# Forty instead of thirty-two tokens by gathered rows in the expert layer of a fused two-block kernel

## The chip, the cores and the metric

The kernel runs on one core of one Trainium2 chip. The metric is the device time of one execution in microseconds (us). A core has TensorE (PE in the profile, with PEld for its weight loads), VectorE (DVE), ScalarE (ACT), GpSimd (POOL) and SyncE (SP), which here issues the loads.

## The reference

Two transformer blocks on 256 tokens of 1024 features, in f32. The change touches one layer of the first block, a product-key expert layer with 128 x 128 = 16384 experts. Each token has 8 heads with 16 chosen experts each, so 128 chosen experts per token:

```python
def peer_ffn(h, w_query, sub_keys, expert_u, expert_v):
    ...
        q = (hc @ w_query).reshape(chunk, PEER_HEADS, PEER_QDIM)
        s1 = jnp.einsum('thd,nd->thn', q[..., :half], k1)
        s2 = jnp.einsum('thd,nd->thn', q[..., half:], k2)
        v1, i1 = lax.top_k(s1, PEER_TOPK)
        v2, i2 = lax.top_k(s2, PEER_TOPK)
        ...                                   # the best 16 of the pairs: eidx, and their softmax g
        u = jnp.take(expert_u, eidx, axis=0)
        a = jnp.einsum('thkd,td->thk', u, hc)
        act = jax.nn.gelu(a, approximate=False) * g
        vv = jnp.take(expert_v, eidx, axis=0)
        return jnp.einsum('thk,thkd->td', act, vv)
```

The rest (two attentions, gates, projections, a second block) is the same in both kernels.

## The kernel before

Every weight slot of 128 x 1024 f32 comes by one DMA into one of four buffers `RAW` (`sp_program`; the load of slot n waits for slot n-4 to be split), is split by ACT into a high part (`split`, L1100) and by DVE (L1547) or POOL (L2263) into a low part in one of three buffers `SPL`, and PE multiplies high and low parts with the high and low parts of the activations in fp32r. ACT may write slot n only when PE has used slot n-3.

**Two ways through the expert layer.** For the first `W` = 224 tokens the kernel computes all 16384 experts densely: 128 slots of U and 128 slots of V, and a table `GB` of gates that is zero where an expert was not chosen. The last `TG` = 32 tokens are done by rows. The list of their chosen experts (`erow`) stands on 128 partitions, `GROUPS` = 4 groups of 32 chosen experts by 32 tokens, one column per turn. In each of 32 turns an indirect DMA of POOL gathers 128 rows of U (`gather`, L2293) and 128 rows of V (L2296), 4 KB a row. DVE multiplies the rows of U with the tokens' activations and sums (the dot, L2040), ACT takes the gelu and the gate (L1359, L1361), and DVE adds the rows of V times that number to `yrow` (the sum, L2050). Each kind has two buffers, so turn j's gather waits for turn j-2's dot or sum. The odd turns' buffers share memory with `HS`, the split activations, and are free only when the last slot of U is done; so all turns but the first gather are beside V. At the end eight matmuls with `fold` (L933) add `yrow`'s four groups to the dense sums.

**The order of the layer** is one generator, `peer_steps` (L105), that all engines walk:

- U slots 0 to 47 (`ROUTED`): 24 matmuls of 224 columns each. Beside them DVE chooses the experts (`route`, L1861), and from slot 28 (`LISTED`) on it also makes the low parts.
- The step "turn" before slot 46: PE transposes the choice (L913), DVE copies it to `T3f` (L2008), makes the first marks and writes `erow` and `grow` (`chosen`, L1931, eight operations on 32 x 32).
- U slots 48 to 123 beside the gates: one step "g" makes the gates of 4 tokens: DVE marks (L1927), ACT weighs (L1313), PE multiplies (4 matmuls, written as 8 records), ACT and DVE store and apply them (L1374, L1955). 224/4 = 56 such steps are spread over 76 slots (`BESIDE`). A slot here has 8 matmuls of 448 columns (high weights by both parts of the activations) and 8 of 224; ACT copies the second half out (L1329), DVE adds it (L2025) and applies the gates already there (`gated_u`, L1947). U's PSUM ring has three banks, so slot i+3 waits for `gated_u` of slot i, which DVE does in its step i+1.
- U slots 124 to 127, then V slots 0 to 127. A slot of V has 8 matmuls of 448 and 8 of 224 columns; ACT and DVE prepare its other operand `asp` (L1349, L1550).

The turns are tied to slots of V by a table:

```python
def gather_slots():
    return {j * 107 // (TG - 1): j for j in range(TG)}
```

DVE does dot j at slot s of that table and sum j at slot s+2, both after the slot's low part and ahead of `asp`. POOL makes no low parts in these stages. At V slot 32 SP also issues four loads for the second block.

Of the kernel before, what the change touches and what calls it, by code (L numbers as in the profile page):

```python
# [14 lines left out]
TG = 32  # L15
W = T - TG
GROUPS = 128 // TG
# [117 lines left out]
def gather_slots():  # L135

    return {j * 107 // (TG - 1): j for j in range(TG)}

# [135 lines left out]
def build(nc, A):  # L274
# [12 lines left out]
    with ctx:  # L287
# [87 lines left out]
        hrow, grow, erow = RS[:, 0:TG], RS[:, TG:2 * TG], RS[:, 2 * TG:3 * TG].bitcast(u32)  # L375
# [5 lines left out]
        keysT = ar.take("keysT", 256).rearrange("p (a n) -> p a n", a=2)  # L381
# [11 lines left out]
        far = ar.take("far", 256).rearrange("p (a h n) -> p a h n", a=2, h=8)  # L393
# [209 lines left out]
        def pe_program(e):  # L603
# [285 lines left out]
            for what, i in peer_steps():  # L889
                if what == "u":  # L890
# [11 lines left out]
                    if i in (8, 9):  # L902
                        ps = take("scr", "xrow", i - 8)
                        for c in range(4):
                            w.wait_ge(*at("copies"))
                            t = mm(ps[:, c * 128:c * 128 + 128], copies[:, 4 * (i - 8) + c, :], ident)
                        t.then_inc(*up("pe_turn", ("full", "xrow", i - 8)))
                elif what == "turn":
# [12 lines left out]
                elif what == "v":  # L921
# [7 lines left out]
                    if i == NE - 1:  # L929
                        vs, parts_v = [i - 1, i], last_v + parts_v  # L930
                        w.wait_ge(*at("yrow", TG - 1))
                        for c in range(8):
                            mm(bank(VB[c])[:, 2 * W:W + 256], yrow[:, c * 128:c * 128 + 128], con("fold"), False, False, True)  # L933
# [153 lines left out]
        def act_program(e):  # L1087
# [208 lines left out]
            beside = gather_slots()  # L1296
# [20 lines left out]
            for what, i in peer_steps():  # L1317
                if what == "u":
# [16 lines left out]
                    if i == 6:  # L1335
                        w.wait_ge(*at("hn", 1, 7))
                        e.activation(copies.rearrange("p c (g t) -> p c g t", g=GROUPS),
                                     HF[:, :, W:T].unsqueeze(2).to_broadcast([128, 8, GROUPS, TG]),
                                     ACT.Copy).then_inc(*up("act_copy", ("copies",)))
                    if i in (9, 10):  # L1340
                        w.wait_ge(*at("full", "xrow", i - 9))
                        e.activation(xrow[:, 512 * (i - 9):512 * (i - 9) + 512], psum("xrow", i - 9),
# [7 lines left out]
                elif what == "v":  # L1350
# [5 lines left out]
                    if i - 1 in beside:  # L1356
                        j = beside[i - 1]
# [180 lines left out]
        def dve_program(e):  # L1538
# [976 lines left out]
```

## Time and profile before

| | |
|---|---|
| median of 3 runs | 1320.63 us (1319.66 to 1322.25) |
| the profiled execution | 1322.05 us, span 1319.9 us |
| busy share of the span | PE 99%, PEld 95%, DVE 77%, ACT 63%, POOL 39% |
| moved by DMA | 268.35 MB, mean 203 GB/s |
| mean granted TensorE clock | 0.997 of full speed |

A span is the time from the first to the last instruction of the core. Matmuls are pipelined and their ends are modelled, so a busy PE is not PE at its peak. The rate of PE is better read from the starts of ACT's splits (L1100): where one waited for PE, it starts just after PE is done with a slot, and the distance between two such starts is PE's time for a slot.

### The profile page before, as it was taken

How to read it: one execution, taken by the hardware profiler on the slowest of the kernel's cores; microseconds unless marked ns; L12 is line 12 of the kernel's file. 1: busy time of each engine (PE TensorE's matmuls, PEld its weight loads, DVE VectorE, ACT ScalarE, POOL GpSimd, SP SyncE). 2: the span in 40 equal slices, each digit the busy share in tenths (PEclk: the TensorE clock that was granted, in tenths of full speed). 3: DMA queues.
4: the chain of work that ended last, by engine and by line, in shares of the span. 5: the costliest groups of instructions: out<-in, count | busy, mean ns of one | idle time of the engine just before them, and what ended most of it. 6: DMA issues, size and time to landing. Idle time of an engine off the chain costs nothing.

```text
span 1319.9 us, 24819 instructions
## 1 busy us (share of the span) xinstructions
PE 1304.3 (99%) x9818; PEld 1258.0 (95%) x9818; DVE 1014.1 (77%) x1845; ACT 827.4 (63%) x1679; POOL 521.2 (39%) x252
## 2 busy tenths in 40 slices
PE   9999999999999999999999999999999999999998
PEld 8999899999999999999989999999999999999997
DVE  4573645859999888899978798998867845899943
ACT  6564646545455888887855565555566666666653
POOL 3745566678901000000014444324204463794442
PEclk9999999999999999999999999999999999999999
DMA  8433345455656555454569999999865544556552
GB/s 305 136 110 127 123 134 178 164 175 178 197 187 203 195 172 164 162 173 162 162 228 325 352 351 330 335 338 329 301 208 172 168 136 130 184 170 194 187 192 96
DMA packets 74298, 268.35 MB, mean 203 GB/s; under 512 B 8252, under 2 KB 8636, under 8 KB 74184
## 3 DMA queue, kind: packets, MB, share of 16 engines
q1 hardware_dynamic: 64968, 233.22, 52.6%
q0 software_dynamic: 9216, 33.56, 6.9%
q8 instruction: 78, 1.28, 0.4%
q14 instruction: 36, 0.29, 0.1%
HBM read 265.70 MB, written 1.05 MB: 202 GB/s over the span
## 4 chain that ended last, share of the span: by engine, by line
PE 85%; DVE 10%; ACT 2%; DMA 1%; issue 1%; POOL 0%; SPq 0%; DVEq 0%; ACTq 0%
PE PS L619 85%; ACT SPL L1100 1%; DVE SPL L1547 1%; DMA RAW<-in_ev 1%; DVE ixu L1837 1%; DVE Ssc L1831 1%; DVE ixu L1828 1%; PE PS L762 1%; DMA RAW<-in_dense 1%; DVE bias L1626 0%; DVE top L1834 0%; DVE top L1825 0%; DVE HF L1564 0%; DVE qpc L1877 0%; DVE HS L1576 0%
## 5 line engine op out<-in xcount | busy, mean ns | idle before, releaser
L1100 ACT ACTIVATE SPL<-RAW 128x1024 fp32r<-128x1024 f32 x429 | 453.8, 1059 | 367.9 <-PE PS L619 345.6
L619 PE MATMUL PS<-HS,SPL 128*128 128x224 f32 (+2 forms) x3968 | 531.9, 292 | 3.3 <-DVE GB L1947 1.7
L619 PEld LDWEIGHTS PS<-HS,SPL 128*128 128x128 f32 x3968 | 502.7, 189 | 15.3 <-DVE SPL L1547 4.1
L2263 POOL TENSOR_TENSOR SPL<-RAW,SPL 128x1024 fp32r<-128x1024 f32 x149 | 361.7, 2433 | 261.3 <-ACT SPL L1100 261.3
L1547 DVE TENSOR_TENSOR SPL<-RAW,SPL 128x1024 fp32r<-128x1024 f32 x280 | 345.1, 1234 | 145.4 <-ACT SPL L1100 142.9
L619 PE MATMUL PS<-asp,SPL 128*128 128x448 f32 (+1 forms) x2048 | 322.1, 319 | 1.6 <-DVE GB L1947 1.2
L619 PEld LDWEIGHTS PS<-asp,SPL 128*128 128x128 f32 x2048 | 307.5, 190 | 15.8 <-DVE GB L1947 1.7
L2293 POOL DMA_INDIRECT rows<-in_er,RS x16 | 27.9, 1744 | 284.0 <-PE PS L619 250.2
L619 PE MATMUL PS<-HXb,SPL 128*128 128x256 f32 x720 | 89.3, 284 | 0.6 <-issue 0.5
L619 PEld LDWEIGHTS PS<-HXb,SPL 128*128 128x128 f32 x720 | 87.4, 188 | 1.3 <-issue 1.0
L1313 ACT ACTIVATE oh<-oh,T3f 128x128 f32<-128x128 f32 x224 | 71.4, 404 | 0.0
L1927 DVE TENSOR_TENSOR oh<-CC,T3f 128x1024 f32<-128x1024 f32 x56 | 68.3, 1220 | 0.1
L619 PE MATMUL PS<-actT,SPL 128*128 128x256 f32 x528 | 62.7, 281 | 0.0
L619 PEld LDWEIGHTS PS<-actT,SPL 128*128 128x128 f32 x528 | 62.6, 188 | 0.0
L2293 POOL DMA_INDIRECT urow<-in_er,RS x16 | 28.8, 1797 | 85.7 <-DVE RS L1939 59.1
L619 PE MATMUL PS<-oh 128*128 128x128 f32 x448 | 60.1, 277 | 0.1
L619 PEld LDWEIGHTS PS<-oh 128*128 128x128 f32 x448 | 54.2, 191 | 2.0 <-ACT oh L1313 0.2
L1550 DVE TENSOR_TENSOR asp<-GB,asp 128x224 fp32r<-128x224 f32 x128 | 49.5, 387 | 2.1 <-ACT asp L1349 2.1
L1349 ACT ACTIVATE asp<-GB 128x224 fp32r<-128x224 f32 x128 | 47.8, 374 | 1.9 <-DVE GB L1955 1.9
L2296 POOL DMA_INDIRECT rows<-in_ev,RS x16 | 29.5, 1845 | 47.0 <-DVE rows L2050 46.7
L619 PE MATMUL PS<-HXa,SPL 128*128 128x256 f32 x384 | 46.9, 282 | 0.4 <-POOL SPL L2263 0.4
L619 PEld LDWEIGHTS PS<-HXa,SPL 128*128 128x128 f32 x384 | 45.9, 188 | 0.7 <-issue 0.6
(296 smaller groups left out, 1509.1 us busy)
## 6 DMA issues: line engine op xcount, KB each, us to landing
RAW<-in_dense SPq DMA_DIRECT2D x176, 512.0 KB, 3.6
RAW<-in_eu SPq DMA_DIRECT2D x128, 512.0 KB, 3.5
RAW<-in_ev SPq DMA_DIRECT2D x128, 512.0 KB, 6.1
bias<-in_nab SPq DMA_DIRECT2D x2, 768.0 KB, 8.2
XT<-in_xT SPq DMA_DIRECT2D x4, 256.0 KB, 6.3
out_y<-HF SPq DMA_DIRECT2D x4, 256.0 KB, 2.2
c<-in_c SPq DMA_DIRECT2D x1, 960.0 KB, 9.1
c<-in_c SPq DMA_DIRECT2D x1, 512.0 KB, 4.7
```

What stands on the lines that cost most here:

```text
L619: return e.matmul(out, l, r, start=start, stop=stop, skip_group_check=skip)
L762: t = e.transpose(ps[:, j, a * 128:a * 128 + 128], probs_of(tag, i)[:, a * 256 * chunks + c * 256 + j * 128: a * 256 * chunks + c * 256 + ...
L1100: e.activation(spl(n)[0], raw(n), ACT.Copy).then_inc(*up("act_high", ("hi", n)))
L1313: q = e.activation(oh[m % 2][:, 1, j, :], oh[m % 2][:, 1, j, :], ACT.Copy, scale=T3f[:, 2, 4 * m + j:4 * m + j + 1])
L1349: e.activation(asp[i % 4][:, 0:W], GB[:, i, :], ACT.Copy).then_inc(*up("act_part", ("ahi", i)))
L1547: e.tensor_tensor(lo, raw(n), hi.bitcast(f32), ALU.subtract).then_inc(*up("dve_low", ("lo", n)))
L1550: return e.tensor_tensor(lo, x, hi.bitcast(f32), ALU.subtract).then_inc(*up("dve_part", *keys))
L1828: e.max_index(it[:, 0:8], vt[:, 0:8], v).then_inc(*up("dve_top", ("where1", k)))
L1927: e.tensor_tensor(oh[m % 2], con("iota").unsqueeze(1).unsqueeze(1).to_broadcast([128, 2, 4, 128]), T3f[:, 0:2, 4 * m:4 * m + 4].unsqueeze( ...
L2263: e.tensor_tensor(lo, raw(n), hi.bitcast(f32), ALU.subtract).then_inc(*up("pool_low", ("lo", n)))
L2293: e.indirect_dma_start(urow[j % 2], None, A["er"], rows_).then_inc(*up(f"urow{j % 2}", ("urow", j), by=16))
L2296: e.indirect_dma_start(vrow[j % 2], None, A["ev"].rearrange("a b c -> (a b) c"), rows_).then_inc(*up(f"vrow{j % 2}", ("vrow", j), by=16))
```

## The change

`TG` goes from 32 to 40 and `W` from 224 to 216. There are now 3 groups of 40 tokens, 120 rows a turn, and 128/3 rounded up = 43 turns. There are 54 steps "g" over the same 76 slots. Every operand that had 224 or 448 columns has 216 or 432.

Fourteen of U's dots (`EARLY`) move beside the gates: dot e follows U slot 56 + e*58//13, slots 56 to 114, with buffers (`urow[0]` and `vrow[0]`) that do not share memory with `HS`. Their gelu is one operation, their gate another. The other 29 dots stand at V slots 0, 4, ... 112, the 43 sums at V slots 2 + j*115//42, that is 2, 4, 7, 10, ... 117. POOL issues U's and V's gathers in the order in which their buffers come free.

The list no longer fits groups of 32 partitions. DVE writes it with token rows to `listed` and clears and fills `shifted_ident`; PE brings it to its 120 partitions with three matmuls after slot 46; DVE copies the two results (`chosen`, now two operations).

```diff
-TG = 32
+TG = 40
 W = T - TG
-GROUPS = 128 // TG
+GROUPS = 3
+ROWED = TG * GROUPS
+TURNS = -(-128 // GROUPS)
+EARLY = 14
...
+def early_slots():
+
+    return {ROUTED + 8 + e * 58 // (EARLY - 1): e for e in range(EARLY)}
...
+def dot_slots():
+
+    return {4 * (j - EARLY): j for j in range(EARLY, TURNS)}
...
+def sum_slots():
+
+    return {2 + j * 115 // (TURNS - 1): j for j in range(TURNS)}
...
+def gather_order():
...
+    dots, sums = {j: s for s, j in dot_slots().items()}, {j: s for s, j in sum_slots().items()}
+    free = [(dots[j - 2], "u", j) for j in range(EARLY + 2, TURNS)]
+    free += [(sums[j - 2], "v", j) for j in range(2, TURNS)]
+    return [("u", EARLY + 1), ("v", 1)] + [(what, j) for _, what, j in sorted(free)]
...
+                    if i == ROUTED - 2:
+                        ps = take("scr", "listed", 0)[:, 0:2 * TURNS].rearrange("p (b n) -> p b n", b=2)
+                        w.wait_ge(*at("listed"))
+                        for g in range(GROUPS):
+                            n = min(TURNS, 128 - TURNS * g)
+                            t = mm(ps[:, :, 0:n], shifted_ident[:, 80 - TG * g:208 - TG * g],
+                                   listed[:, :, TURNS * g:TURNS * g + n], g == 0, g == GROUPS - 1, True)
+                        t.then_inc(*up("pe_turn", ("full", "listed", 0)))
...
+                    if i == 0:
+                        w.wait_ge(*at("dot", EARLY - 1))
+                        e.activation(hrow[:, 0:EARLY], hrow[:, 0:EARLY], ACT.Gelu).then_inc(*up("act_row", ("hgelu", "early")))
...
+            def list_rows():
+
+                e.memset(shifted_ident, 0.0).then_inc(*up("dve_pick", ("cleared",)))
+                e.scalar_tensor_tensor(listed[:, 0], sel[:, 1, 1, :], 128.0, sel[:, 0, 1, :],
+                                       ALU.mult, ALU.add).then_inc(*up("dve_pick", ("listed0",)))
+                w.wait_ge(*at("cleared"))
+                e.tensor_copy(shifted_ident[:, 80:80 + TG], ident[:, 128 - TG:128]).then_inc(*up("dve_pick", ("shifted_ident",)))
+                w.wait_ge(*at("selected"))
+                e.tensor_copy(listed[:, 1], sel[:, 2, 1, :]).then_inc(*up("dve_pick", ("listed",)))
...
             def chosen():
...
-                for g in range(GROUPS):
-                    c = slice(TG * g, TG * g + TG)
-                    r = slice(TG * g, TG * g + TG)
-                    e.scalar_tensor_tensor(erow[r, 0:TG], sel[128 - TG:128, 1, 1, c], 128.0, sel[128 - TG:128, 0, 1, c],
-                                           ALU.mult, ALU.add).then_inc(*up("dve_pick", ("erow",)))
-                    e.tensor_copy(grow[r, :], sel[128 - TG:128, 2, 1, c]).then_inc(*up("dve_pick", ("grow",)))
+                w.wait_ge(*at("full", "listed", 0))
+                ps = psum("listed", 0)[0:ROWED]
+                e.tensor_copy(erow, ps[:, 0:TURNS]).then_inc(*up("dve_pick", ("erow",)))
+                e.tensor_copy(grow, ps[:, TURNS:2 * TURNS]).then_inc(*up("dve_pick", ("grow",), ("ev", "listed", 0)))
...
+                    if i in early_at:
+                        dot(early_at[i], early[early_at[i] % 2])
...
-                if j >= 2:
+            def gather_v(j):
+
+                if j == 0:
+                    w.wait_ge(*at("dot", EARLY - 1))
+                elif j >= 2:
                     w.wait_ge(*at("yrow", j - 2))
...
+                if what == "u" and ROUTED + 3 <= i < ROUTED + 3 + EARLY:
+                    gather_early(i - ROUTED - 3)
                 if (what, i) == ("v", 0):
+                    gather_u(EARLY)
+                    gather_v(0)
                     w.wait_ge(*at("used", EXPERT + NE - 1))
-                    for j in range(1, TG):
-                        gather(j)
+                    for kind, j in gather_order():
+                        if kind == "u":
+                            gather_u(j)
+                        else:
+                            gather_v(j)
```

**The change-over at the step "turn", on DVE.** Before (L1920 ends the choice, L2008 copies it, L1927 makes marks, `RS` holds `erow` and `grow`):

```order
L1920 TENSOR_TENSOR sel<-sel,ssum 128x128 x2
L1547 TENSOR_TENSOR SPL<-RAW,SPL 128x1024 x2
L2008 COPY T3f<-PS 128x3x128 x2
L1927 TENSOR_TENSOR oh<-CC,T3f 128x1024
L1937 SCALAR_TENSOR_TENSOR RS<-sel 32x32
L1939 COPY RS<-sel 32x32
```

Now (`keysT` holds `shifted_ident`, `far` holds `listed`; all lines have moved):

```order
L1958 TENSOR_TENSOR sel<-sel,ssum 128x128 x2
L1585 TENSOR_TENSOR SPL<-RAW,SPL 128x1024 x2
L1971 MEMSET keysT 128x208
L1972 SCALAR_TENSOR_TENSOR far<-sel 128x128
L1975 COPY keysT<-CC 128x40
L1977 COPY far<-sel 128x128
L2061 COPY T3f<-PS 128x3x128 x2
L1965 TENSOR_TENSOR oh<-CC,T3f 128x1024
L1983 CAST RS<-PS 120x43
L1984 COPY RS<-PS 120x43
L1965 TENSOR_TENSOR oh<-CC,T3f 128x1024
```

Four operations stand ahead of the copies of the choice, and two stand where eight (four pairs) were, behind the first marks.

**Beside the gates, on DVE, in the change** (L1585 low part, L2078 sum of U's halves, L1999 `gated_u`, L1990 an early dot, L1965 marks, L2007 gates applied):

```order
L1585 TENSOR_TENSOR SPL<-RAW,SPL 128x1024
L2078 TENSOR_TENSOR PS<-PS,rows 128x216
L1999 TENSOR_TENSOR GB<-GB,PS 128x32
L1990 SCALAR_TENSOR_TENSOR vrow,RS<-vrow,rows 120x1024
L1965 TENSOR_TENSOR oh<-CC,T3f 128x1024
L2007 TENSOR_TENSOR GB<-GB,PS 128x60x4
```

Without the dot these are the rows of before; it stands ahead of the marks and of the next slot's low part.

**In V, on DVE, in the change** (L1588 `asp`, L2105 a sum):

```order
L1585 TENSOR_TENSOR SPL<-RAW,SPL 128x1024
L1990 SCALAR_TENSOR_TENSOR rows,RS<-rows 120x1024
L2105 SCALAR_TENSOR_TENSOR rows<-rows,RS 120x1024
L1588 TENSOR_TENSOR asp<-GB,asp 128x216
L1585 TENSOR_TENSOR SPL<-RAW,SPL 128x1024
```

Here, at V slot 4, a dot and a sum fall into one slot, which the table before never did; it happens at 11 slots (4, 12, 32, 40, 48, 56, 64, 84, 92, 100, 108).

## Rows read from the trace of the kernel before

**Rows 1.** The page: engines, and the chain that ended last by engine.

```profile
PE 1304.3 (99%) x9818; PEld 1258.0 (95%) x9818; DVE 1014.1 (77%) x1845; ACT 827.4 (63%) x1679; POOL 521.2 (39%) x252
PE 85%; DVE 10%; ACT 2%; DMA 1%; issue 1%; POOL 0%; SPq 0%; DVEq 0%; ACTq 0%
```

**Rows 2.** The timeline of ACT, V slots; start us, us, instruction, idle before, releaser.

```profile
840.18 1.06 ACT L1100 ACTIVATE SPL<-RAW 128x1024 fp32r<-128x1024 f32 x1 [1.17 <-PE PS L619]
...
905.35 1.06 ACT L1100 ACTIVATE SPL<-RAW 128x1024 fp32r<-128x1024 f32 x1 [1.17 <-PE PS L619]
```

**Rows 3.** The same view, U slots of 24 matmuls of 224 columns.

```profile
327.88 1.06 ACT L1100 ACTIVATE SPL<-RAW 128x1024 fp32r<-128x1024 f32 x1 [1.38 <-PE PS L619]
...
357.36 1.06 ACT L1100 ACTIVATE SPL<-RAW 128x1024 fp32r<-128x1024 f32 x1 [1.38 <-PE PS L619]
```

**Rows 4.** The same view, the last projection, 24 matmuls of 256 columns a slot.

```profile
1207.00 1.06 ACT L1100 ACTIVATE SPL<-RAW 128x1024 fp32r<-128x1024 f32 x1 [1.46 <-PE PS L619]
...
1249.40 1.06 ACT L1100 ACTIVATE SPL<-RAW 128x1024 fp32r<-128x1024 f32 x1 [0.47 <-PE PS L619]
```

**Rows 5.** The timeline of PE at the fold.

```profile
995.62 1.94 PE L619 MATMUL PS<-CC,rows 128*128 128x32 f32 x16
997.40 5.26 PE L619 MATMUL PS<-asp,SPL 128*128 128x448 f32 x32
```

**Rows 6.** The timeline of ACT beside the gates.

```profile
627.00 1.06 ACT L1100 ACTIVATE SPL<-RAW 128x1024 fp32r<-128x1024 f32 x1 [0.49 <-PE PS L619]
...
630.39 1.06 ACT L1100 ACTIVATE SPL<-RAW 128x1024 fp32r<-128x1024 f32 x1 [0.49 <-PE PS L619]
```

**Rows 7.** The timeline of DVE in the same stretch.

```profile
628.09 1.22 DVE L1547 TENSOR_TENSOR SPL<-RAW,SPL 128x1024 fp32r<-128x1024 f32 x1
...
629.53 0.34 DVE L1947 TENSOR_TENSOR GB<-GB,PS 128x184 f32<-128x184 f32 x1
629.78 1.22 DVE L1927 TENSOR_TENSOR oh<-CC,T3f 128x1024 f32<-128x1024 f32 x1
630.92 0.61 DVE L1955 TENSOR_TENSOR GB<-GB,PS 128x444 f32<-128x444 f32 x1
631.49 1.22 DVE L1547 TENSOR_TENSOR SPL<-RAW,SPL 128x1024 fp32r<-128x1024 f32 x1
...
633.99 1.23 DVE L1547 TENSOR_TENSOR SPL<-RAW,SPL 128x1024 fp32r<-128x1024 f32 x1 [0.72 <-ACT SPL L1100]
```

**Rows 8.** Windows, DVE alone: stretch, its length, busy, clock, DMA share, GB/s.

```profile
544.00:604.00 60.00, 54.49 (x84) 1.00 0.50 167
604.00:664.00 60.00, 55.36 (x85) 1.00 0.51 167
```

**Rows 9.** The timeline of DVE: a dot, and what starts after it.

```profile
683.70 1.22 DVE L2040 SCALAR_TENSOR_TENSOR urow<-urow,rows 128x1024 f32<-128x1024 f32 x1
...
684.85 0.39 DVE L1550 TENSOR_TENSOR asp<-GB,asp 128x224 fp32r<-128x224 f32 x1
```

**Rows 10.** The change-over at "turn": timelines of PE and of DVE.

```profile
417.56 5.60 PE L619 MATMUL PS<-HS,SPL 128*128 128x224 f32 x48
423.22 1.13 PE L619 MATMUL PS<-oh 128*128 128x128 f32 x8
...
419.48 1.02 DVE L2008 COPY T3f<-PS 128x384 f32<-128x384 f32 x2
```

**Rows 11.** The timeline of PE at the end of U.

```profile
671.97 5.25 PE L619 MATMUL PS<-HS,SPL 128*128 128x448 f32 x32 [1.06 <-DVE GB L1947]
```

**Rows 12.** Waits from 666 to 1000 us: total us, times, longest.

```profile
ACT SPL L1100 <- PE PS L619: 109.5, 109, 2.0
ACT SPL L1100 <- DMA RAW<-in_ev: 18.9, 14, 3.5
```

**Rows 13.** V's gathers: from issue to landing, us.

```profile
DMA to landing us min/median/max: 5.6/8.3/9.6
```

**Rows 14.** A window in V, DVE alone, columns as in rows 8.

```profile
820.00:870.00 50.00, 45.99 (x71) 1.00 0.94 332
```

More of the change, by code:

```diff
@@ L380, in build @@
         ar.take("before", ROUTED * W)
-        keysT = ar.take("keysT", 256).rearrange("p (a n) -> p a n", a=2)
+        keys_ = ar.take("keysT", 256)
+        keysT = keys_.rearrange("p (a n) -> p a n", a=2)
+        shifted_ident = keys_[:, 0:208]
         qpc = ar.take("qpc", 4096)
@@ L392, in build @@
         abf = ar.take("abf", 1024).rearrange("p (b a h n) -> p b a h n", b=4, a=2, h=8)
-        far = ar.take("far", 256).rearrange("p (a h n) -> p a h n", a=2, h=8)
+        far_ = ar.take("far", 256)
+        far = far_.rearrange("p (a h n) -> p a h n", a=2, h=8)
+        listed = far_.rearrange("p (b n) -> p b n", b=2)
         eqs = [ar.take(f"eqs{i}", 2048).rearrange("p (h k j) -> p h k j", h=8, k=16) for i in range(2)]
@@ L1295, in act_program @@
                                      ACT.Copy).then_inc(*up("act_copy", ("ev", "sc", c4, a)))
-            beside = gather_slots()
+            dots = dot_slots()
             def gelu(i):
@@ L1355, in act_program @@
                     cur[0] += 1
[L1356 to L1357 removed]
+                    if i == 0:
+                        w.wait_ge(*at("dot", EARLY - 1))
+                        e.activation(hrow[:, 0:EARLY], hrow[:, 0:EARLY], ACT.Gelu).then_inc(*up("act_row", ("hgelu", "early")))
+                    if i - 1 in dots:
+                        j = dots[i - 1]
                         w.wait_ge(*at("dot", j))
@@ L1998, in angles @@
                     yield
-            routing, turning, beside = route(), angles(), gather_slots()
+            routing, turning, early_at, dots, sums = route(), angles(), early_slots(), dot_slots(), sum_slots()
             for _ in range(4):
@@ L2034, in dve_program @@
                     cur[0] += 1
-                    if i in beside:
-                        j = beside[i]
-                        w.wait_ge(*at("urow", j))
-                        w.wait_ge(*at("ev", "xrow", 1))
-                        u_ = urow[j % 2]
-                        e.scalar_tensor_tensor(u_, u_, 1.0, xrow, ALU.mult, ALU.mult,
-                                               accum_out=hrow[:, j:j + 1]).then_inc(*up("dve_row", ("dot", j)))
-                    if i - 2 in beside:
-                        j = beside[i - 2]
+                    if i == 1:
+                        w.wait_ge(*at("hgelu", "early"))
+                        e.tensor_tensor(hrow[:, 0:EARLY], hrow[:, 0:EARLY], grow[:, 0:EARLY], ALU.mult).then_inc(
+                            *up("dve_row", *[("hrow", j) for j in range(EARLY)]))
+                    if i in dots:
+                        dot(dots[i], urow[dots[i] % 2])
+                    if i in sums:
+                        j = sums[i]
+                        y_, v_ = yrow[0:ROWED], vrow[j % 2][0:ROWED]
                         w.wait_ge(*at("vrow", j))
```

48 lines of the change are left out of this document (30 added, 18 removed).

## The prediction

> **What bounds the kernel now.** I read the page first. PE is busy 99% of the span and the chain of waits runs 85% through it [rows 1]. But a busy PE is only a PE with work in hand, so I took its rate from the timeline of ACT, where each split that waited for PE starts as PE ends a slot. In V 26 slots take 905.35 - 840.18 = 65.17 us: 2.507 us a slot, with no slot longer than another [rows 2]. DVE is busy 45.99 of 50 us in such a stretch [rows 14], but over V it is ACT that waits for PE (109 times, 109.5 us in all, against 14 times for a load) [rows 12], and DVE behind ACT. So V goes by PE's columns. The same reading gives 2.680 us for a U slot of 24 matmuls of 224 columns (29.48 us for 11 slots) [rows 3], and beside the gates 3.39 us for a slot with one step "g" [rows 6], which is 2.507 + 0.88 for the gate's 8 records.
>
> Then I asked what narrower operands give PE. 24 matmuls of 256 columns take 2.827 us (42.40 us for 15 slots), 117.8 ns each [rows 4]; of 224 columns 111.7 ns [rows 3]. At 2.4 GHz 32 columns are 13.3 ns, and only 6.1 ns were saved. And in the fold a record with 32 columns takes 1.78 us / 16 = 111 ns [rows 5], as much as a gate's record with 128 (0.88/8 = 110 ns) [rows 2, 6]. So there is a floor of about 111 ns from one matmul to the next, whatever the columns, and a matmul of 224 columns is already on it. A pair of V (448 and 224) takes 2507/8 = 313.3 ns [rows 2]: 111.7 for the short one, 201.6 for the long one (448 columns are 186.7), which is far above the floor.
>
> The Trainium skill (TensorE: Matmul & The Clock Gate, section LDWEIGHTS) says why there may be a floor: loading weights takes the number of weight columns divided by 1.2 in ns, an estimate of 106.7 ns for 128, however few columns are then multiplied; this speaks against a change that narrows the short matmuls. Its section on the back-to-back issue gap has N/2.4 + 2.5 ns instead, by which each of the 16 matmuls would gain. The rows fit the first at 224 columns and neither at 448.
>
> **The change part by part.** The sum is against the profiled execution, 1322.05 us with a span of 1319.9 us; it lies 1.4 us above the median of the runs, 1320.63, so the same difference is taken from the median.
>
> *U slots 0 to 47.* Each matmul goes from 224 to 216 columns, on the floor [rows 3]: 0. From above, if the columns counted, 48 x 24 x 3.33 ns = 3.8 us; but DVE chooses the experts at the same time and PE would then wait for it, so even then little of it would be left. I take 0.
>
> *The change-over.* After slot 46 PE gets three f32 matmuls, 6 records of 111 ns [rows 5]: 0.67 us. Ahead of its copies to T3f (2 of them 1.02 us) [rows 10] DVE gets four small operations of 208, 128, 40 and 128 columns. No row shows them; the copies, at 384 columns, are about 0.5 us each, so they are between 0.1 and 0.4 us each: 0.4 to 1.6 us, I take 0.8. Gate 0 hangs on both: slots 46 and 47 begin at 417.56 and need 48 x 111.7 ns = 5.36 us, so they end at 422.92, and gate 0 begins at 423.22, 0.3 us late: ACT's weighing, behind DVE's marks, ends last [rows 3, 10]. DVE's 0.8 us therefore counts in full and hides PE's 0.67. **+0.8 us.** The eight operations that become two come after the first marks and delay nobody; with the marks first, their loss or gain is 0.
>
> *Beside the gates.* A slot's 8 long matmuls lose 16 columns, 6.67 ns each: 0.053 us a slot. The 8 short ones are on the floor. 76 slots: **-4.1 us**. Two gates less: 2 x 0.88 = **-1.8 us**. The 14 dots: each takes DVE 684.85 - 683.70 = 1.15 us [rows 9]. Is there room? From 628.09 to 631.49 DVE works 3.40 us without a gap for a slot with a gate, exactly PE's 3.39; it rests only at a slot without one, 0.72 us [rows 6, 7]. Over 60 us it rests 5.5 us, later 4.6 [rows 8]. New, a window of 60 us becomes 58.6 us (5.9 us off four of them), has half a gate less (0.5 x 1.71 us of marks and gates applied, 629.78 to 631.49 [rows 7]) and 4.3 dots, 4.9 us. 5.5 - 1.4 + 0.9 - 4.9 = 0.1 us of rest: DVE is full, though not over. Its slack towards PE is small too: in step i+1 `gated_u` ends 629.53 + 0.34 - 627.00 = 2.87 us after PE ended slot i+1, and PE wants that bank after one more slot and at least one gate, 2.45 + 0.88 = 3.33 us. So 0.46 us are free, and a dot is 1.15. From below, no stall: in the first half DVE rests at every gate. From above, each of the 14 dots pays 1.15 - 0.46 = 0.69 us: 9.7 us. I take half of that for the 6 dots of the full stretch and little for the rest: **+2 us**. The 14 gathers themselves go at half the DMA's load (0.51) [rows 8]: 0.
>
> *U slots 124 to 127.* PE waits there for `gated_u` (1.06 us in this row, three such waits) [rows 11], a time that ACT and DVE set. Narrower matmuls give 0.
>
> *V.* 128 slots x 0.053 = **-6.8 us**, to 2.453 us a slot. DVE's dots and sums here, 64, become 29 + 43 = 72. Per slot up to 117: low part 1.14 and `asp` 0.3 (starts of rows one behind the other), dots 0.25 x 1.15, sums 0.37 x 1.2: 2.17 us of 2.45, 88%. Where dot and sum meet, DVE has 3.8 us of work, 1.3 over a slot; buffers give it two slots less ACT's 1.06 and its own 1.14, 2.5 us, and the next slots are lighter. DMA: 524 KB + 0.617 x 492 KB in 2.453 us is 337 GB/s, where 332 GB/s were a share of 0.94 [rows 14]. The gathers: V's two buffers now turn in 5 or 6 slots, 12.3 us at the least; a sum (1.3), perhaps a gather of U in front on POOL (2.0) and 8.3 us to landing, at most 9.6 [rows 13], are 11.6, at most 12.9. So DVE will now and then wait for rows, which it never did before, and the loads will be late oftener than 14 times [rows 12]. From below 0; from above half a microsecond at each of 11 meetings and 1 us around SP's four extra loads, 6 us; I take **+0.7 us**, nearest to the 14 late loads of before, none of which stopped the steady stretch. The fold gets 40 columns for 32: still the floor, 0.
>
> Sum: 0.8 - 4.1 - 1.8 + 2 - 6.8 + 0.7 = -9.2 us: 1312.9 against the profiled execution, 1311.4 against the median. I say **1311.5 us**. Each dense slot gets cheaper on PE, and the eleven more turns are paid for by DVE, POOL and DMA.
>
> **The rivals.**
>
> *Short matmuls follow their columns.* If the 111.7 ns were streaming with an overhead and not a floor, all 16 matmuls of a slot gain 3.33 or 6.67 ns: 0.080 us a slot, 204 slots, 5.4 us more: **1306 us**. For it: a pair's 313.3 ns is also 672 columns plus 2 x 16.7 ns [rows 2]. Against it: 256 and 224 columns differ by less than half of their columns [rows 3, 4], and 32 columns cost what 128 do [rows 5]. 18%. By the Trainium skill's issue gap (page and section above) this case would be the one to come.
>
> *DVE becomes the bound beside the gates.* All 14 dots stall PE by 0.69 us, or the dots' gathers and loads add to it: 9.7 us instead of 2: **1319 us**, no change that can be told. For it: 3.40 us without a gap [rows 7]. Against it: the first half of the stage is lighter. 11%.
>
> *Slower: V's gathers arrive late.* Place: POOL's one queue and V's two buffers. A buffer's cycle is a sum, the issue and the landing; with landing L it is L + 1.3 + up to 2.0 us, and two turns must go through in 2 x 2.74 slots = 13.4 us on average. It decides from L = 10.1 us on, against 8.3 now, 9.6 the most [rows 13]. The load would do it if DMA, at 0.94 [rows 14], cannot give 337 GB/s. At L = 11.5 the cycle is 0.7 us a turn too long: 43 x 0.7 = 30 us less what dots in other slots leave of the 2.0, say 20 us, for a gain of 9: **1331 us**. The Trainium skill (DMA: Bandwidth & Descriptors, section Why a DMA increments its semaphore by 16 and not by 1) says that a transfer of 120 rows goes to 15 of the 16 DMA engines, 8 rows each, since 16 does not divide it; by this a gather would land no sooner than one of 128 rows. No row of before shows a gather of 120. 9%.
>
> **How the numbers follow.** My forecast, 1308 to 1316 us: 55%. The rivals 18, 11 and 9%; that the stalls cancel most of the gain elsewhere, 1316 to 1322: 7%. The range takes in the faster rival and its margin, and the stalls of the gates up to 8 us: 1304 to 1318.5 us, which leaves out the slower rival, part of the two middling ones, and a remainder. A measurement tells 0.2%, 2.6 us, from no change. Faster than 1318.0: 55 + 18 + a third of the next two = 79%; the same: 11%; slower: 10%.
>
> **What would show it.** In the changed profile: splits in V 2.453 us apart (the first rival: 2.427; no gain: 2.507); U slots still 2.680; gate 0 begins about 0.8 us later behind slot 47; beside the gates DVE about 96% busy and waits of PE for DVE's `gated_u`, behind a dot, of some 2 us together; in V waits of DVE for the gathers below 2 us, landing about 8.5 us, PE waiting for low parts below 1 us in all. Wrong would be: U slots of 2.60 us, PE waits of over 5 us beside the gates, or landing over 10 us.

## The result, and the profile after

The changed kernel takes **1384.83 us** (median of 6 runs, 1382.52 to 1392.79) against 1321.01 us of the kernel before beside it (6 runs): a ratio of 1.0489, 95% interval 1.0471 to 1.0507. The forecast was 1311.5 us and a range of 1304 to 1318.5; the time lies far outside it, on the other side of no change. The slower rival named the right stage, but its 1331 us are not near either.

The page of the changed kernel, span, engines, DMA queues (packets, MB, share of the 16 engines) and chain:

```profile
span 1385.1 us, 24849 instructions
PE 1316.0 (95%) x9808; PEld 1264.0 (91%) x9808; DVE 1033.6 (75%) x1873; ACT 819.9 (59%) x1665; POOL 543.5 (39%) x274
q1 hardware_dynamic: 64968, 233.23, 53.4%
q0 software_dynamic: 12384, 42.28, 12.2%
PE 54%; DVE 19%; DMA 17%; ACT 4%; POOL 3%; issue 2%; SPq 0%; DVEq 0%; ACTq 0%
```

Against [rows 1] the chain has 17% of DMA in it that was not there, and PE's part of it is down to 54%. The queues of the kernel before, on its page:

```profile
q1 hardware_dynamic: 64968, 233.22, 52.6%
q0 software_dynamic: 9216, 33.56, 6.9%
```

q0 carries the gathers, q1 the loads. The gathered bytes grew by 26%; the time that they hold the DMA engines nearly doubled: 0.122 x 1385.1 = 169 us of all 16 engines, against 0.069 x 1319.9 = 91. Spread over the rows fetched (86 x 120 and 64 x 128) that is 0.122 x 16 x 1385.1 / 10320 = 262 ns for a row of 4 KB, against 178 ns.

Where the time went shows in a table by stage, read from the starts of ACT's splits, as in the prediction. Slots are counted over U and V; the last five columns are experiments told of below.

```
us                      before   after   padded  dots   free    loads   both
                                                 short  slots   spread
U slot 3 to 48          123.32  123.25  123.24  123.24  123.26  123.29  123.26
slot 48 to 50             6.01    7.13    7.14    7.13    7.13    7.12    7.12
slot 50 to 127          245.67  249.30  249.27  240.24  240.29  249.22  240.30
slot 127 to V's end     326.66  386.71  325.03  322.83  324.19  320.76  319.47
```

V and what stands between U's last slot and V take 60 us more. The change-over takes 1.1 us more, the stage beside the gates 3.6 us more, where it was to take 3.9 less. The other stretches nearly cancel (the start 0.7 us less, behind V 1.1 us more). The table is of one execution of each kernel, and those of the changed and the padded kernel do not lie at their medians: differences of medians are given beside it.

V: the timeline of ACT, two rows from the middle and two from the end.

```profile
813.38 1.06 ACT L1135 ACTIVATE SPL<-RAW 128x1024 fp32r<-128x1024 f32 x1 [2.88 <-DMA RAW<-in_ev]
816.83 1.06 ACT L1135 ACTIVATE SPL<-RAW 128x1024 fp32r<-128x1024 f32 x1 [1.70 <-DMA RAW<-in_ev]
...
1054.81 1.06 ACT L1135 ACTIVATE SPL<-RAW 128x1024 fp32r<-128x1024 f32 x1 [1.12 <-PE PS L646]
1057.27 1.06 ACT L1135 ACTIVATE SPL<-RAW 128x1024 fp32r<-128x1024 f32 x1 [1.12 <-PE PS L646]
```

At the end, with the gathers over, a slot takes 2.46 us, the 2.453 us of the forecast; in the middle it takes 3.45 us and ends with a load. The waits of the whole program for DMA, with the stretch 770 to 950 (length, DVE's busy time, granted clock, DMA share, GB/s) and the landing of V's gathers:

```profile
ACT SPL L1135 <- DMA RAW<-in_ev: 168.5, 88, 9.4
```

```profile
770.00:950.00 180.00, 132.99 (x185) 0.95 1.01 275
```

```profile
DMA to landing us min/median/max: 5.8/11.0/13.6
```

Before, ACT waited 14 times and 18.9 us for loads [rows 12], and a gather landed in 8.3 us [rows 13]. Now DMA is full (share 1.01) and yet moves 275 GB/s, where 332 GB/s were a share of 0.94 [rows 14]. The loads suffer with the gathers: SP's loads of V land in 9.0 us on the page after, and they are what ACT waits for:

```profile
RAW<-in_ev SPq DMA_DIRECT2D x128, 512.0 KB, 9.0
```

U beside no gate, same view, first and last of 11 slots:

```profile
327.23 1.06 ACT L1135 ACTIVATE SPL<-RAW 128x1024 fp32r<-128x1024 f32 x1 [1.38 <-PE PS L646]
...
356.71 1.06 ACT L1135 ACTIVATE SPL<-RAW 128x1024 fp32r<-128x1024 f32 x1 [1.38 <-PE PS L646]
```

29.48 us / 11 = 2.680 us, to the hundredth what stood there with 224 columns [rows 3]. The fold's 16 records now have 40 columns, on PE's timeline:

```profile
1059.83 1.95 PE L646 MATMUL PS<-CC,rows 120*128 120x40 f32 x16 [0.20 <-DVE SPL L1585]
1061.61 4.74 PE L646 MATMUL PS<-asp,SPL 128*128 128x432 f32 x29
```

1.78 us / 16 = 111 ns, as with 32 columns [rows 5]. The floor is there.

The change-over, on PE and on DVE:

```profile
416.90 2.91 PE L646 MATMUL PS<-HS,SPL 128*128 128x216 f32 x24
420.01 0.90 PE L646 MATMUL PS<-far,keysT 128*128 128x86 f32 x6 [0.20 <-DVE T3f L2061]
420.70 2.92 PE L646 MATMUL PS<-HS,SPL 128*128 128x216 f32 x24
423.45 0.73 PE L646 MATMUL PS<-oh 128*128 128x128 f32 x5
```

```profile
418.89 0.23 DVE L1971 MEMSET keysT<- 128x208 f32 x1
...
419.40 1.01 DVE L2061 COPY T3f<-PS 128x384 f32<-128x384 f32 x2
```

The four small operations took 0.51 us together. But it is PE that ends last: slot 46, at 111.7 ns a matmul, would be over at 419.58, its six records of the list wait for `T3f` and begin at 420.01, and they push slot 47 by 0.69 us more. The 0.43 and the 0.69 us are the 1.1 us. Gate 0 follows slot 48's split of ACT by 6.87 us (423.45 - 416.58) where it was 5.97 (423.22 - 417.25).

Beside the gates PE stops behind each dot. PE and DVE around one of them:

```profile
615.55 1.06 PE L646 MATMUL PS<-oh 128*128 128x128 f32 x8
617.44 2.69 PE L646 MATMUL PS<-HS,SPL 128*128 128x432 f32 x16 [0.82 <-DVE GB L1999]
619.96 1.07 PE L646 MATMUL PS<-oh 128*128 128x128 f32 x8
```

```profile
612.77 1.22 DVE L1990 SCALAR_TENSOR_TENSOR vrow<-vrow,rows 120x1024 f32<-120x1024 f32 x1
...
613.91 1.22 DVE L1965 TENSOR_TENSOR oh<-CC,T3f 128x1024 f32<-128x1024 f32 x1
615.05 0.59 DVE L2007 TENSOR_TENSOR GB<-GB,PS 128x420 f32<-128x420 f32 x1
615.55 1.22 DVE L1585 TENSOR_TENSOR SPL<-RAW,SPL 128x1024 fp32r<-128x1024 f32 x1
616.68 0.39 DVE L2078 TENSOR_TENSOR PS<-PS,rows 128x216 f32<-128x216 f32 x1
616.97 0.32 DVE L1999 TENSOR_TENSOR GB<-GB,PS 128x164 f32<-128x164 f32 x1
```

The gate ends on PE at 616.6. The `gated_u` in line 1999, which sets the next bank free, ends at 617.3, since the dot has pushed marks, gate, low part and sum back by 1.14 us. From the gate's first record to the next slot's it takes 617.44 - 615.55 = 1.89 us, where 620.78 - 619.96 = 0.82 us are usual: this dot costs 1.07 us, more than the 0.82 us of its row, because the ends of PE's records are modelled. And the waits of this stage (423 to 690), total, times, longest:

```profile
PEld PS L646 <- DVE SPL L1585: 9.9, 12, 1.3
PE PS L646 <- DVE GB L1999: 8.9, 14, 1.2
```

Three of the 14 waits in the second line stand in the last slots of U, as before the change [rows 11]. The other 11, 5.9 us in all, come each behind one dot: behind five of the first seven (0.19 to 0.55 us in PE's rows) and behind six of the last seven (0.57 to 0.86 us). Two of the three dots without one are those of slots 82 and 96, the only ones of the 14 in a slot without marks and gate.

### The profile page after: what moved, and what is told of

It reads as the page before. It is cut to its first block, busy times and chain, and to the rows that moved or that the text cites. A ratio compares the mean times of both kernels' runs of the same rounds, so it can differ in the third digit from the quotient of the medians.

```text
span 1385.1 us, 24849 instructions
## 1 busy us (share of the span) xinstructions
PE 1316.0 (95%) x9808; PEld 1264.0 (91%) x9808; DVE 1033.6 (75%) x1873; ACT 819.9 (59%) x1665; POOL 543.5 (39%) x274
## 3 DMA queue, kind: packets, MB, share of 16 engines
q0 software_dynamic: 12384, 42.28, 12.2%
## 4 chain that ended last, share of the span: by engine, by line
PE 54%; DVE 19%; DMA 17%; ACT 4%; POOL 3%; issue 2%; SPq 0%; DVEq 0%; ACTq 0%
PE PS L646 53%; DMA RAW<-in_ev 16%; DVE SPL L1585 5%; ACT SPL L1135 4%; POOL SPL L2318 2%; DVE oh L1965 1%; DVE rows L2105 1%; DMA rows<-in_ev,RS 1%; POOL HF L2397 1%; DVE urow L1990 1%; DVE PS L2078 1%; DVE ixu L1875 1%; DVE Ssc L1869 1%; DVE ixu L1866 1%; PE PS L789 1%
## 5 line engine op out<-in xcount | busy, mean ns | idle before, releaser
L646 PE MATMUL PS<-HS,SPL 128*128 128x216 f32 (+2 forms) x3968 | 528.4, 292 | 8.6 <-DVE GB L1999 7.7
L646 PEld LDWEIGHTS PS<-HS,SPL 128*128 128x128 f32 x3968 | 502.8, 190 | 18.9 <-DVE SPL L1585 11.0
L1585 DVE TENSOR_TENSOR SPL<-RAW,SPL 128x1024 fp32r<-128x1024 f32 x280 | 345.0, 1234 | 191.0 <-ACT SPL L1135 189.3
L646 PE MATMUL PS<-asp,SPL 128*128 128x432 f32 (+1 forms) x2048 | 334.5, 323 | 49.2 <-DVE SPL L1585 47.7
L646 PEld LDWEIGHTS PS<-asp,SPL 128*128 128x128 f32 x2048 | 313.2, 193 | 70.1 <-DVE SPL L1585 60.8
L2366 POOL DMA_INDIRECT vrow<-in_ev,RS x22 | 36.2, 1648 | 94.2 <-DVE rows L2105 75.8
L2348 POOL DMA_INDIRECT urow<-in_er,RS x7 | 12.1, 1728 | 145.3 <-DVE urow L1990 86.5
L1965 DVE TENSOR_TENSOR oh<-CC,T3f 128x1024 f32<-128x1024 f32 x54 | 65.9, 1221 | 0.0
L2366 POOL DMA_INDIRECT rows<-in_ev,RS x21 | 34.6, 1647 | 65.0 <-DVE rows L2105 63.1
L2356 POOL DMA_INDIRECT rows<-in_er,RS x14 | 19.8, 1413 | 82.6 <-DVE rows L1990 46.4
L1588 DVE TENSOR_TENSOR asp<-GB,asp 128x216 fp32r<-128x216 f32 x128 | 48.5, 379 | 1.9 <-ACT asp L1384 1.9
L1384 ACT ACTIVATE asp<-GB 128x216 fp32r<-128x216 f32 x128 | 47.0, 367 | 1.9 <-DVE GB L2007 1.9
```

The lines of the kernel that those rows point to most:

```text
L646: return e.matmul(out, l, r, start=start, stop=stop, skip_group_check=skip)
L1384: e.activation(asp[i % 4][:, 0:W], GB[:, i, :], ACT.Copy).then_inc(*up("act_part", ("ahi", i)))
L1585: e.tensor_tensor(lo, raw(n), hi.bitcast(f32), ALU.subtract).then_inc(*up("dve_low", ("lo", n)))
L1588: return e.tensor_tensor(lo, x, hi.bitcast(f32), ALU.subtract).then_inc(*up("dve_part", *keys))
L1965: e.tensor_tensor(oh[m % 2], con("iota").unsqueeze(1).unsqueeze(1).to_broadcast([128, 2, 4, 128]), T3f[:, 0:2, 4 * m:4 * m + 4].unsqueeze( ...
L2356: e.indirect_dma_start(urow[j % 2][0:ROWED], None, A["er"], bass.IndirectOffsetOnAxis(ap=erow[:, j:j + 1], axis=0)).then_inc(*up(f"urow{j ...
```

## The experiments

Two questions were open: is V's loss the 120 rows of a gather, or the number and place of the gathers; and is the loss beside the gates the 14 dots, their gathers, or something else. All ratios are against the kernel before on the same chip, with their 95% interval.

**Padded gathers.** The changed kernel, but each gather fetches 128 rows. The list gets indices on all 128 partitions; 8 rows more, row 0 of the tables each time, are fetched and not used.

```diff
-        erow = RS[0:ROWED, 2 * TURNS:3 * TURNS].bitcast(u32)
+        erow = RS[:, 2 * TURNS:3 * TURNS].bitcast(u32)
...
-                ps = psum("listed", 0)[0:ROWED]
+                ps = psum("listed", 0)
...
-                e.indirect_dma_start(vrow[j % 2][0:ROWED], None, A["ev"].rearrange("a b c -> (a b) c"),
+                e.indirect_dma_start(vrow[j % 2], None, A["ev"].rearrange("a b c -> (a b) c"),
```

> The changed kernel with every gather of 128 rows again; the 8 rows more are row 0 of the tables, fetched and not used. Theory A (a gather of 120 rows is badly spread over the DMA engines and slows its own packets and the loads beside it): the splits in V come 2.45 us apart, V's loads land in 6 to 7 us instead of 9, DMA moves 340 GB/s or more, and the kernel takes 1310 to 1316 us, faster than before. Theory B (72 gathers beside V are simply too much for DMA, or POOL's one queue and the two buffers bring them too late): 8 more rows a turn make it worse or leave it, 1385 us or more, at the same 270 to 285 GB/s.

Measured: 1326.93 us (6 runs, 1322.76 to 1329.50), ratio 1.0044 (1.0029 to 1.0060). The bytes went up and 58 us went away. Theory A is right on the gathers, but the time is 11 us over its range: more was wrong than the 120 rows. Its queues on the page, and its stretch 770 to 950:

```profile
q1 hardware_dynamic: 64968, 233.23, 52.3%
q0 software_dynamic: 12384, 45.09, 9.6%
```

```profile
770.00:950.00 180.00, 165.00 (x228) 1.00 0.95 343
```

343 GB/s at a share of 0.95, with the same 86 gathers, slots, buffers and waits. U's stage and the change-over are as in the changed kernel (table), so the 120 rows are worth 386.71 - 325.03 = 61.7 us in V (58 us by the medians of the whole time): all of the loss there, and a little gain that they hid. A slot of V is 2.453 us:

```profile
779.40 1.06 ACT L1135 ACTIVATE SPL<-RAW 128x1024 fp32r<-128x1024 f32 x1 [1.12 <-PE PS L646]
...
789.21 1.06 ACT L1135 ACTIVATE SPL<-RAW 128x1024 fp32r<-128x1024 f32 x1 [1.12 <-PE PS L646]
```

(9.81 us for 4 slots.) But V's end comes only 1.6 us sooner than before, measured from slot 127, where 6.1 were forecast. What is missing shows a little earlier in V. The timeline of SP, and that of ACT behind it:

```profile
747.52 0.63 SPq L618 DMA_DIRECT2D pF<-in_pT  x1
748.19 0.43 SPq L619 DMA_DIRECT2D c<-in_c  x1
748.66 1.47 SPq L620 DMA_DIRECT2D posi<-in_pos  x1
750.18 0.75 SPq L621 DMA_DIRECT2D poolw<-in_poolw  x1
```

```profile
754.44 1.06 ACT L1135 ACTIVATE SPL<-RAW 128x1024 fp32r<-128x1024 f32 x1 [1.12 <-PE PS L646]
762.82 1.06 ACT L1135 ACTIVATE SPL<-RAW 128x1024 fp32r<-128x1024 f32 x1 [7.05 <-DMA RAW<-in_ev]
```

SP issues its four late loads in a row, 1.6 MB, and the load of V behind them makes ACT wait 7.05 us. PE then has nothing to do, it is busy 0.91 of the 3.30 us from 762.8, and after that its granted clock is 0.50, the lower level of 1.2 GHz, from 766.1 to 769.5: 13 matmuls in 3.30 us, where the 5.4 us after it hold 37.

**120 rows in the kernel before.** No other part of the change: its gathers, dots and sums take 120 of their 128 rows, in the same slots. What the other 8 rows hold is left out of the result; so it is in the runs with 112, 96 and 64 rows.

```diff
-                rows_ = bass.IndirectOffsetOnAxis(ap=erow[:, j:j + 1], axis=0)
+                rows_ = bass.IndirectOffsetOnAxis(ap=erow[0:120, j:j + 1], axis=0)
...
-                e.indirect_dma_start(urow[j % 2], None, A["er"], rows_).then_inc(*up(f"urow{j % 2}", ("urow", j), by=16))
+                e.indirect_dma_start(urow[j % 2][0:120], None, A["er"], rows_).then_inc(*up(f"urow{j % 2}", ("urow", j), by=16))
```

> The kernel before with its 32 turns where they were, but only the first 120 of each turn's 128 rows are gathered, multiplied and summed (the other 8 chosen experts of the last tokens are left out). Theory A: V gets slower by about as much as in the change, its loads land in 9 us or so, a time of 1340 to 1380 us. Theory B: fewer bytes, so the same time as before or a little less, 1318 to 1321 us, loads landing in 6.2 us.

Measured: 1376.17 us, ratio 1.0417 (1.0399 to 1.0435). Less to fetch and less to compute, and 55 us slower; from slot 127 to V's end it takes 384.24 us, 57.6 more than before. 266 ns a row; the same stretch:

```profile
770.00:950.00 180.00, 131.58 (x184) 0.98 1.00 263
```

Taken together, the first two runs settle what costs V its 60 us: taking 120 rows away from the change cures it, putting 120 rows into the kernel before brings it.

**112 rows in the kernel before.** The same edit with 112. 16 divides 112, so this asks whether 120 is bad because it does not divide evenly.

> As the run with 120 rows, but with 112, 16 times 7 (16 chosen experts of the last tokens are left out). If it is the number of engines that a transfer is spread over that decides (15 for 120 rows, 16 for 112), this is as fast as before, 1318 to 1321 us. If it is that each engine's rows no longer fall on the same partitions as in a load of 128 rows, it is as slow as the run with 120 rows, 1340 us or more. Theory B expects no change here either way.

Measured: 1345.32 us, ratio 1.0183 (1.0166 to 1.0201). 243 ns a row. Even division is not enough: by the count of engines alone, which is what the rule of the Trainium skill cited in the prediction gives (16 divides 112), this run would have cost nothing.

**96 and 64 rows in the kernel before.** The same edit again, twice.

> As the runs of the kernel before with 120 and 112 rows a turn, now 96 (6 rows for each of 16 engines; 32 chosen experts of the last tokens are left out). Theory S (any transfer that is not 128 rows writes partitions other than those its engines have in a load of 128, and packets of both slow each other down): packets take clearly more than the 159 ns of before, DMA stays under 310 GB/s and the time over 1325 us, in spite of a quarter less to gather. Theory K (only numbers that leave engines out, or rows per engine near 7, are slow): 1317 to 1322 us.

> As before with 64 rows a turn, half of the gathers' bytes (the other 64 chosen experts of the last tokens are left out). Theory S: packets still slow (over 190 ns in the mean for the gathers), but so few that V goes by PE again: 1318 to 1325 us. Theory K: 1317 to 1320 us, packets as before.

Measured: 96 rows 1342.24 us, ratio 1.0159 (1.0140 to 1.0177), 258 ns a row; 64 rows 1324.40 us (8 runs, 1320.38 to 1328.99), ratio 1.0032 (1.0018 to 1.0046), 253 ns a row. With half of the gathered bytes the kernel is still not faster than with all of them. The stretch with 64 rows:

```profile
770.00:950.00 180.00, 161.09 (x227) 1.00 0.99 271
```

0.99 of the DMA engines for 271 GB/s, where before 0.94 gave 332 [rows 14]. The durations of the single packets of 4 KB in this stretch, worked out from the trace, say the same of every version (median and mean, ns; "loads+slots" is the run "Both" below):

```
                rows   gathers (q0)   loads (q1)
before          128     159  179       159  184
padded          128     159  179       159  180
loads+slots     128     159  179       159  175
after           120     271  267       213  223
before, 120     120     272  270       232  237
before, 112     112     245  242       209  220
before, 96       96     265  259       205  221
before, 64       64     244  256       194  232
```

Two groups without anything between them. A gather of 128 rows runs at 159 ns a packet (median), as do the loads beside it. One of 120, 112, 96 or 64 slows its own rows by 63 to 92 ns in the mean and the loads' packets beside it by 36 to 53 ns; 120 rows are the slowest on both queues, and the three smaller sizes differ little. Since the loads are two thirds of the traffic, their 40 ns are worth about as much as the gathers' 90: in this stretch of the changed kernel 7588 x 39 ns = 296 us of engine time against 4245 x 88 = 374, together 670 of the 2880 that 16 engines have.

Why it is so no run shows, as none tells which engine carried a packet, or into which partition. The Trainium skill (SBUF — State Buffer, section Door 1: The DMA port swizzle) says that a transfer's bandwidth depends on how many of the 16 ports into the memory its partitions reach, and that the partitions 0 to 63 reach half of them. The Trainium skill (DMA: Bandwidth & Descriptors, section The descriptor swizzle) has each engine of a 128-row transfer writing a port of its own. Engines that meet at a port would look like these rows: packets longer, not more numerous, and on both queues. The traces agree in that, and in that 64 rows are slow. But by the port table of the first section 96, 112 and 120 rows reach all 16 ports, so the number of ports alone would have them fast, and the rows say 242 to 267 ns against 179. How their rows are dealt out over the engines neither section says. That engines meet at a port stays a reading that fits and was not tried further.

**Short dots beside the gates.** The padded version, and its 14 early dots multiply 8 columns instead of 1024. The gathers stay.

```diff
+                n = 8 if j < EARLY else 1024
-                e.scalar_tensor_tensor(u_[0:ROWED], u_[0:ROWED], 1.0, xrow[0:ROWED], ALU.mult, ALU.mult,
+                e.scalar_tensor_tensor(u_[0:ROWED, 0:n], u_[0:ROWED, 0:n], 1.0, xrow[0:ROWED, 0:n], ALU.mult, ALU.mult,
```

> The run with padded gathers, but the 14 dots beside the gates multiply 8 columns instead of 1024 (their result is wrong, the gathers and all waits stay). Theory D (the dots' 1.15 us each fill DVE and stall PE by about 9 us beside the gates): the last U slot is split 8 to 10 us earlier than in e1, its distance from the first gate is what 2.454 us a slot and 0.89 us a gate give, and the time falls to 1316 to 1319 us. Rival G (it is the 14 gathers, their traffic or POOL's issues, that cost the time there): it stays at 1325 to 1329 us.

Measured: 1315.56 us, ratio 0.9958 (0.9941 to 0.9974). The stage is 240.24 us instead of 249.27 (table): the dots' time on DVE costs 9.0 us, what theory D said; the whole time is 0.4 us under its range. The gathers are all still there. What is left of the waits:

```profile
PE PS L646 <- DVE GB L2000: 3.0, 3, 1.2
```

Those three are the ones that stood there before the change [rows 11].

**Dots in slots without a gate.** The padded version, with whole dots, each moved to a slot in which DVE has no marks and no gate to do.

```diff
-    return {ROUTED + 8 + e * 58 // (EARLY - 1): e for e in range(EARLY)}
+    return {i: e for e, i in enumerate((54, 58, 61, 65, 68, 72, 75, 79, 82, 86, 89, 92, 96, 99))}
```

> The run with padded gathers, but the 14 early dots stand at 14 slots of U without a gate step, 54 to 99, where DVE rests 0.7 us, and earlier on the whole. Theory D: about 5 to 8 us of the 9 come back, 1319 to 1323 us. Rival G: the gathers are the same, so 1325 to 1329 us.

Measured: 1317.90 us, ratio 0.9970 (0.9959 to 0.9981), 1.1 us under the range; the stage takes 240.29 us. The full dots cost nothing there: as much is won as by taking them away. They also stand earlier on the whole, but that is not it: in the changed kernel five of the first seven dots stop PE, and the two in slots without a gate, 82 and 96, do not. The waits are the same three:

```profile
PE PS L646 <- DVE GB L1999: 3.0, 3, 1.2
```

So it is not how busy DVE is. In slots 50 to 127 it works 224.6 us in the best version (below) and 224.9 in the changed one, 93% and 90% of the stage. In the 60 us from 544 the best version's DVE works 59.06, the changed one's 56.18:

```profile
544.00:604.00 60.00, 59.06 (x97) 1.00 0.64 211
```

The fuller one has the shorter stage, and no wait of PE for `gated_u` in these 60 us. What decides is whether 1.15 us come into the one slot whose slack is 0.46.

**Late loads spread.** The padded version, with SP's burst taken apart: `pF` stays where it was, `c2` goes in 4 pieces, and these and the other two loads are set 4 slots apart and more.

```diff
-                if n == EXPERT + NE + LATE + NSPL + NRAW:
+                late = n - (EXPERT + NE + LATE + NSPL + NRAW)
+                if late == 0:
...
-                    e.dma_start(c2, A["c2"]).then_inc(*up("c2", ("c2",), by=16))
+                if late in (6, 10, 14, 18):
+                    c = slice(120 * late - 720, 120 * late - 240)
+                    e.dma_start(c2[:, c], A["c2"][:, c]).then_inc(*up("c2", ("c2",), by=16))
+                if late == 22:
...
+                if late == 26:
```

> The run with padded gathers, but SP's four loads for the second block (1.6 MB at V slot 32) are issued as seven, spread over 26 slots. Theory L (DMA at 0.95 has no room for the burst, so the loads of V fall behind by 3 to 4 us around V slots 32 to 40): this stretch runs at 2.45 us a slot and the time falls by 2 to 5 us, 1322 to 1325 us. If V's loss in e1 is spread over the stage instead (V's gathers late), it stays at 1325 to 1329 us.

Measured: 1319.60 us, ratio 0.9985 (0.9975 to 0.9994). From slot 127 to V's end it takes 320.76 us, 4.3 less than the padded version; by the medians 7.3 us are won, more than the 2 to 5 expected. The clock has a part in that: the 3.4 us at 0.50 behind the burst are not in this trace. Why the medians lie further apart than the two traces no run shows; the mean granted clock of the padded runs is 0.994 to 0.997, that of these 0.996 to 0.999.

**Both.** Free slots and spread loads, on the padded version.

> Padded gathers, early dots at gate-free slots and the spread loads together. If the three causes add up: 1315 to 1319 us, faster than before by 2 to 6 us. If one hides behind the other, 1320 us or more, no faster than before.

Measured: **1309.71 us** (4 runs, 1309.40 to 1310.56), ratio 0.9911 (0.9894 to 0.9927): better than both kernels, and computing all that they compute. It is 5 us under the range expected; the two gains, 9.0 and 7.3 us off 1326.93, would give 1310.6, so they add up. Its waits in V for loads and its stretch 770 to 950:

```profile
ACT SPL L1140 <- DMA RAW<-in_ev: 37.9, 26, 3.0
```

```profile
770.00:950.00 180.00, 165.36 (x231) 1.00 0.95 351
```

DMA gives 351 GB/s here, more than the 337 that the forecast asked of it. 26 loads are late, none by more than 3.0 us, and V keeps its pace.

**Spread loads in the kernel before.** That same edit to the kernel before alone, to see whether the last version's gain is the change's or the edit's.

> The kernel before with only SP's four loads for the second block spread over 26 slots of V. In its trace V lost about 0.8 us there, so it gains no more than that: 1319.5 to 1321.5 us. If it gains 3 us or more, the gain of the combined run is largely this and not the change's.

Measured: 1319.67 us, ratio 0.9993 (0.9984 to 1.0002). It gives the kernel before nothing that can be told, since the burst had cost it nearly nothing (no wait of V over 3.5 us [rows 12]). The 0.9% of the version above is the work of the change, once its three losses are out.

## Why the prediction was wrong

**The step that failed** is in the part on V: "DMA: 524 KB + 0.617 x 492 KB in 2.453 us is 337 GB/s, where 332 GB/s were a share of 0.94". It counted bytes and took a gather of 120 rows to cost DMA fifteen sixteenths of one with 128. The page gives 262 ns a row against 178, and it slows the loads too, so DMA's full share gives 275 GB/s, where the rows of before work out to 332 / 0.94 = 353. The term was +0.7 us with a bound of 6 from above; it measured 66.8 (386.71 - 326.66 + 6.8), of which the 120 rows are 61.7 (386.71 - 325.03), and 120 rows alone bring 57.6 to the kernel before. The nearest rows for the bound were all of gathers with 128 rows, and beside their number and order the shape was what the change altered in the gathers. I looked at it only where they landed, as a question of when and not of how fast; the one sentence on 15 of 16 engines stood with the slower rival and was given no price.

**The slower rival** had the stage, the first sign (landing 11.0 us, past its 10.1) and the condition ("if DMA, at 0.94 [rows 14], cannot give 337 GB/s") right. Its mechanism, POOL's one queue and two buffers that turn too slowly, is not what ended the slots: ACT waited 88 times for SP's loads (168.5 us), and the other engines behind it. For a gather DVE waited once in all of V:

```profile
DVE rows L2105 <- DMA rows<-in_ev,RS: 1.0, 1, 1.0
```

It priced 20 us; it was three times that. Of the prediction's three signs of being wrong two came: the landing over 10 us, and waits of PE over 5 us beside the gates (5.9).

**Short matmuls on the floor: right.** 2.680 us with 216 columns as with 224, 111 ns for a fold's record with 40 columns as with 32. The rival in which short matmuls follow their columns is out: V's slots are 2.453 us and not 2.427. The formula N/2.4 + 2.5 ns, which the prediction takes from the Trainium skill (TensorE: Matmul & The Clock Gate, section Back-to-back issue gap), is given there for a single isolated matmul, and as too low at few columns in a stream of weight loads and matmuls, which is what runs here; it was no ground for this rival. The long ones gave what they were priced at: V's slot went from 2.507 to 2.453 us, the stage beside the gates, without stalls, from 245.67 to 240.3, which is -5.4 where -5.9 was the sum.

**The change-over: nearly right.** +1.1 us against +0.8. The four operations of DVE were less than said (0.51 us, not 0.8), but PE's records, which I had hidden behind them, wait for `T3f` and so come on top instead of beside.

**The stalls beside the gates: mis-sized.** +2 us was taken, "half of that for the 6 dots of the full stretch and little for the rest"; they cost 9.0 (249.27 - 240.24), close to the bound of 9.7 from above. That is 0.82 us for each of the 11 dots behind which PE stopped, against 1.15 - 0.46 = 0.69 for each of 14. The mechanism was right and the slack nearly; the discount for a lighter first half was not, as five of its seven dots stop PE: a rest that comes later in the stage, or even one slot later, does not help the low part and `gated_u` of this slot. The rival "DVE becomes the bound beside the gates", given 11%, had the price of this stage right. Its name was not: DVE is no bound, since the same dots cost nothing in other slots.

**V without the 120 rows: half right.** (A small slip first: two slots less 1.06 and 1.14 us are 2.7 us and not 2.5; nothing hangs on it.) -6.8 us and +0.7 give 320.6 us from slot 127 to V's end; with padded gathers it is 325.03, and with the loads spread as well 320.76, so the 4.4 us that were missing are nearly all the one term that I named and priced too low, "1 us around SP's four extra loads". That burst meets a DMA with little to spare and costs a wait of 7.05 us, and behind it 3.4 us at half the clock. The forecast that DVE "will now and then wait for rows" did not come true, but for the one wait above.

The sum by what was measured, for the span: start -0.7, U slots -0.1, change-over +1.1, gates -5.4 + 9.0, V and before it 60.1 (of which 61.7 for 120 rows and -1.6 for the rest), behind V +1.1: +65.1 us, where the spans, 1319.9 and 1385.1, are 65.2 apart.

## What to carry to other kernels

Cost a gather by its shape and not by its bytes: fetch 128 rows even if some are thrown away, and where a change alters the shape of a transfer in a stage where DMA is at 0.9, measure that transfer before trusting any row of the old shape. A short operation put on an engine with little slack is priced slot by slot, against the buffer that is waited for there; the average rest over 60 us says nothing, and moving the operation to a slot where that engine has one job less can make it free. A burst of loads that a kernel carries without harm can cost several microseconds once the stage's pace is raised, and can be spread at no cost.

## What the runs showed of the hardware that was not expected

- Indirect gathers into 120, 112, 96 or 64 partitions take 267, 242, 259 and 256 ns per row of 4 KB (mean, busy DMA), into 128 partitions 179 ns; the loads of 128 partitions beside them go from 175 to 184 ns to 220 to 237 ns. With 64 rows the DMA engines are at 0.99 for 271 GB/s.
- A gather of 120 rows comes with 24 small packets, one of 128, 112, 96 or 64 rows with 16: q0 has 12384 packets both for 86 gathers of 120 rows (86 x 144) and for 86 of 128 (86 x 144), and 8192 for 64 gathers of 112 (64 x 128). The number of packets is thus no sign of the cost.
- Where PE stood waiting for loads in V its granted clock fell now and then to 0.50: in the changed kernel four times, from 740.3, 777.9, 853.0 and 880.3, for 20.5 us in all; for 10.2 us with 96 rows, 6.8 with 120 rows in the kernel before, 3.4 with 112 rows and in the padded versions that keep the burst of late loads, and not at all in V before, with 64 rows, with the loads spread and in the last version. Over 770 to 950 the mean is 0.95 in the changed kernel, 0.98 in the kernel before with 120 rows, 0.99 with 96 and 1.00 in all others. An estimate from these: 20.5 us at half the clock are worth at most 10.2 us and the padded version's 3.4 at most 1.7, so of the 61.7 us the clock can be at most some 10; and the kernel before with 120 rows lost 57.6 us in V with 6.8 us of it.
